# Latent attention in pairs of query blocks, with a split of the turned weights, in a two-block transformer kernel

## The reference, cut to what matters

```python
MLA_HEADS = 8; QK_NOPE = 64; QK_ROPE = 32; V_DIM = 64; Q_RANK = 256; KV_RANK = 128; Q_BLOCK = 128
def mla_attention(c_q, c_kv, k_rope, q_norm_g, w_uq, kv_norm_g, w_ukv, cos, sin):
    q = (rms_norm(c_q, q_norm_g) @ w_uq).reshape(b_, l_, MLA_HEADS, QK_NOPE + QK_ROPE)
    q_nope, q_rope = jnp.split(q, [QK_NOPE], axis=-1)
    q_rope = apply_rope(q_rope, cos[:, None, :], sin[:, None, :])
    kv = (rms_norm(c_kv, kv_norm_g) @ w_ukv).reshape(b_, l_, MLA_HEADS, QK_NOPE + V_DIM)
    k_nope, v = jnp.split(kv, [QK_NOPE], axis=-1)
    k_rope = apply_rope(k_rope, cos, sin)
    # k = [k_nope, k_rope shared by all heads]; q scaled by 96 ** -0.5
    # per query block: causal scores over all keys (the meta tokens too), softmax, times v
y_b = (mla_attention(cq, ckv, kr, ...) * jax.nn.silu(mg)) @ w_out_mla
```

## Time and profile before

| | before |
|---|---|
| median of 3 runs | 2844.04 us (2843.68 to 2848.91) |
| the profiled execution | 2843.15 us |
| its span, first to last instruction | 2841.3 us |
| busy: PE, weight loads (PEld) | 2760.0 us (97%), 2267.9 us (80%) |
| busy: DVE, ACT, POOL | 1026.0, 924.8, 578.6 us |
| mean granted TensorE clock | 0.991 |

### The profile page before, as it was taken

One profiled execution on the slowest core, in us unless ns is written; L12 is line 12 of the kernel. 1 busy time (PEld: TensorE's weight loads), 2 busy tenths in 40 slices (PEclk: granted clock), 3 DMA queues, 4 the chain that ended last, 5 costly groups with the idle time before them and its releaser, 6 DMA issues.

```text
span 2841.3 us, 34234 instructions
## 1 busy us (share of the span) xinstructions
PE 2760.0 (97%) x13644; PEld 2267.9 (80%) x13644; DVE 1026.0 (36%) x1293; ACT 924.8 (33%) x1477; POOL 578.6 (20%) x245
## 2 busy tenths in 40 slices
PE   7999999999999999999999999989999999999999
PEld 6677788898888888777778888867688888888887
DVE  3544423552323222734533665321333212121223
ACT  4455532112212114533434555332432112021122
POOL 1000012222222223221111224231121222222221
PEclk9999999999999999999999999999999999999999
DMA  3000001111111114131112123220021111111112
GB/s 125 14 13 13 15 22 45 51 46 39 43 52 48 46 48 148 38 106 38 38 37 87 46 86 131 100 67 30 23 66 38 45 52 45 52 44 52 45 52 89
DMA packets 42774, 154.50 MB, mean 54 GB/s; under 512 B 4884, under 2 KB 5204, under 8 KB 41896
## 3 DMA queue, kind: packets, MB, share of 16 engines
q1 hardware_dynamic: 37712, 128.11, 14.3%
q10 hardware_dynamic: 4952, 24.82, 2.3%
HBM read 138.04 MB, written 10.67 MB: 52 GB/s over the span
## 4 chain that ended last, share of the span: by engine, by line
PE 87%; DVE 5%; issue 4%; ACT 2%; POOL 1%; DMA 0%; ACTq 0%; DVEq 0%; POOLq 0%
PE ps L594 46%; PE ps L675 18%; PE ps L696 5%; PE ps L799 3%; PE ps L770 2%; PE ps L1108 2%; PE ps L1066 1%; PE ps L788 1%; PE ps L1269 1%; PE ps L1060 1%; DVE fx_tl L2531 1%; PE ps L653 1%; PE ps L1145 1%; PE ps L617 1%; PE ps L1175 1%
## 5 line engine op out<-in xcount | busy, mean ns | idle before, releaser
L506 POOL TENSOR_TENSOR w_lo<-w_raw,w_hi 128x1024 fp32r<-128x1024 f32 x205 | 500.7, 2443 | 2128.2 <-ACT w_hi L1369 2128.1
L594 PE MATMUL ps<-A_hi,w_hi 128*128 128x512 f32 (+1 forms) x1920 | 549.2, 372 | 9.0 <-POOL w_lo L506 3.1
L594 PE MATMUL ps<-A_lo,w_hi 128*128 128x512 f32 (+1 forms) x1920 | 544.7, 370 | 0.0
L594 PE MATMUL ps<-A_hi,w_lo 128*128 128x512 f32 (+1 forms) x1920 | 544.5, 370 | 0.0
L594 PEld LDWEIGHTS ps<-A_hi,w_hi 128*128 128x128 f32 x1920 | 342.1, 189 | 73.2 <-issue 6.2
L594 PEld LDWEIGHTS ps<-A_lo,w_hi 128*128 128x128 f32 x1920 | 343.3, 188 | 61.6
L594 PEld LDWEIGHTS ps<-A_hi,w_lo 128*128 128x128 f32 x1920 | 343.0, 188 | 61.6
L1369 ACT ACTIVATE w_hi<-w_raw 128x1024 fp32r<-128x1024 f32 x205 | 216.2, 1055 | 497.3 <-PE ps L675 342.7
L2599 DVE TENSOR_TENSOR X<-ps,X 128x512 f32<-128x512 f32 x96 | 66.4, 692 | 383.8 <-PE ps L675 305.9
L675 PE MATMUL ps<-w_hi,U_hi 128*128 128x512 f32 x448 | 174.3, 389 | 0.0
L675 PE MATMUL ps<-w_lo,U_hi 128*128 128x512 f32 x448 | 174.3, 389 | 0.0
...
## 6 DMA issues: line engine op xcount, KB each, us to landing
...
```

The lines of the kernel that those rows point to most:

```text
L506: nc.gpsimd.tensor_tensor(w_lo[:, slot, :], w_raw[:, slot, :], w_hi[:, slot, :].bitcast(F32), ALU.subtract).then_inc(w_lo_ready, 1)
L594: last = nc.tensor.matmul(out, w[:, slot, o:o + m], v[:, k, cols] if k is not None else v[:, cols], start=(first and j == 0 and q == 0), s ...
```

## The change

The loop over pairs of heads is written out as 8 heads of 4 steps (`MX_J`), each step a pair of query blocks (2j, 2j+1), j in the order 3, 0, 2, 1.

- Scores stay F32, over 128 rows instead of 96. The query projection, both halves of the rotary part and the scale are taken in one DVE instruction (rows 64 to 127 times cos and ±sin, rows 0 to 63 times 1); the keys hold their rotary part twice, in rows 64 to 95 and 96 to 127, so that the product itself adds the two halves. The mask is a product of an identity with a mask tile on PE. The meta keys stand behind the block's own keys for the first block of a pair, which makes products of 16 columns.
- The turned weights (10 chunks of 512 columns a head) are split into `mx_th` (ACT) and `mx_tl` (DVE), and are the moving operand of the value products, 256 columns for two query blocks; `mx_vs` = [V high|V low] is the stationary one, in fp32r. DVE adds the two halves (`mx_take`). The output comes out turned, so `turn_output` goes.
- The reciprocal of the sums goes through a row, two DMAs (SP) and a product on POOL with the Silu of the gate.
- The projections of the next head, the next pair's values and the gate stand as filler in the steps (`mx_fill`), in one PSUM bank (7) and one free corner (bank 1). The gate comes in two halves of 512 columns, so its Silu is taken in two places a pair.
- A new unit `mla_meta` holds the weights for all meta keys and meta values, which are multiplied once. The keys of a head are one accumulated product over two shifted slices of the weights.
- Elsewhere semaphores are merged; no instruction is changed there but for the slots' parity.

```diff
-    ("mla_heads", 4, (768, 1024)),
+    ("mla_meta", 1, (1024,)),
+    ("mla_heads", 1, (1024,) * 8),
...
+MX_J = (3, 0, 2, 1)
+MX_FIRST = (0, 4, 5, 8)
+MX_CHUNKS = 11
+MX_P_AT = {3: 0, 0: 1968, 2: 0, 1: 1968}
+MX_T_AT = {3: 0, 0: 4, 2: 0, 1: 3}
...
+    for _key in ([("key", 2 * _i + 1), ("query", 2 * _i + 1, 0), ("gate", _i)]
+                 + ([("key", 2 * _i + 2), ("query", 2 * _i + 2, 0), ("query", 2 * _i + 2, 1), ("value", _i + 1, 0), ("value", _i + 1, 1)]
+                    if _i < 3 else [])):
...
+        mx_k = ar("mx_k", 61696, [P, 2, S + 64])[:, :, 64 - META:S + 64]
+        mx_p = ar("mx_p", 70400, [P, 2912])
+        mx_vs = ar("mx_vs", 82176, [P, 2, 10, P], F32R)
+        mx_o = ar("mx_o", 92416, [P, S])
+        mx_th, mx_tl = xr("mx_th", 0, [P, 5, HB], F32R), xr("mx_tl", 10240, [P, 5, HB], F32R)
+        mx_q = xr("mx_q", 20480, [P, 2, S])
+        mx_sil = xr("mx_sil", 28672, [P, S])
...
+                def inverse(h):
+                    rows = slice(64 * (h % 2), 64 * (h % 2) + 64)
+                    sp.wait_ge(mx["row"], h + 1)
+                    sp.dma_start(inv_d[h % 2], mx_row[0:ST, h % 2, :]).then_inc(mx["inv_out"], 16)
+                    sp.wait_ge(mx["inv_out"], 16 * (h + 1))
+                    if h >= 2:
+                        sp.wait_ge(mx["si"], h // 2)
+                    sp.dma_start(mx_inv[rows, :], inv_d[h % 2].rearrange("q p -> (q p)").rearrange("(a c) -> a c", a=1)
+                                 .to_broadcast([64, S])).then_inc(mx["inv_in"], 16)
...
+            lows(0, n0 + 2)
+            for i in range(4):
+                mx_value_low(2 * i)
+                if i:
+                    silu_scaled(i - 1)
+                mx_value_low(2 * i + 1)
+                low(n0 + 2 * i + 2, (n0 + 2 * i + 2) % 2)
+                low(n0 + 2 * i + 3, (n0 + 2 * i + 3) % 2)
+            silu_scaled(3)
...
+            def mx_key(h, bank):
+
+
+                n, e = n0 + 2 * (h // 2), h % 2
+                pe.wait_ge(w_lo_ready, n + 1)
+                for hb in (1, 0):
+                    o, cols = 512 + 128 * e + 64 * (1 - hb), slice(META + hb * HB, META + hb * HB + HB)
+                    for x, (w, v) in enumerate(((w_hi, ckv_hi), (w_hi, ckv_lo), (w_lo, ckv_hi))):
+                        last = nc.tensor.matmul(ps[:, bank, :], w[:, n % 2, o:o + P], v[:, cols], start=(hb == 1 and x == 0),
+                                                stop=(hb == 0 and x == 2))
+                last.then_inc(mx["fd"], 1)
...
+                if h % 2 == 0:
+                    table = ((key, query(0, 7, (mx["v"], 2 * i + 2))), (none, gate(0, 0)), (query(1, 1), gate(0, 1)), (none, gate(1, 0)))
+                    if i == 3:
+                        table = (table[0], (none, none), (query(1, 1), none), (none, gate(0, 0)))
+                elif i < 3:
+                    table = ((key, gate(1, 1)), (none, query(0, 7, (mx["sil"], 2 * i + 2))), (query(1, 1), value(0)), (none, value(1)))
+                else:
+                    table = ((none, gate(0, 1)), (none, gate(1, 0)), (none, gate(1, 1)), (none, none))
+                return table[s]
...
+                for ab in range(2):
+                    qb = 2 * j + ab
+                    qs = slice(qb * P, (qb + 1) * P)
+                    n, flat = (qb + 1) * P, ps[:, 2 * ab:2 * ab + 2, :].rearrange("p a b -> p (a b)")
+                    if ab == 0:
+                        parts = [(c, META + c, min(HB, n - c)) for c in range(0, n, HB)] + [(n, 0, META)]
+                        d = qb * P
+                    elif j < 3:
+                        parts = [(c, c, min(HB, n + META - c)) for c in range(0, n + META, HB)]
+                        d = META + qb * P
+                    else:
+                        parts = [(c, META + c, HB) for c in range(0, n, HB)]
+                        d = qb * P
+                    for at_, c, w in parts:
+                        x, y = max(at_, d), min(at_ + w, d + P)
+                        last = nc.tensor.matmul(flat[:, at_:at_ + w], mx_q[:, e, qs], mx_k[:, e, c:c + w], start=True, stop=x >= y)
+                        if x < y:
+                            last = nc.tensor.matmul(flat[:, x:y], mx_ident[:, :], mx_future[:, x - d:y - d], start=False, stop=True)
...
+                whole = [(kb, t) for kb in range(2 * j + 1) for t in (mx_th, mx_tl)]
+                for x, (kb, t) in enumerate(whole[:1] + [(kb, t) for kb in ("own", "meta_a", "meta_b") for t in (mx_th, mx_tl)] + whole[1:]):
+                    end = MX_T_AT[j] + j
+                    if kb == "own":
+                        v, w, out = mx_vs[:, e, 2 * j + 1, :], t[:, end, 256:384], ps[:, 6, r0 + P:r0 + 256]
+                    elif kb == "meta_a":
+                        v, w, out = mx_vs[:, e, 8, :], t[:, end, 384:512], ps[:, 6, r0:r0 + P]
+                    elif kb == "meta_b":
+                        v, w, out = mx_vs[:, e, 9, :], t[:, end, 384:512], ps[:, 6, r0 + P:r0 + 256]
+                    else:
+                        cols = slice((kb % 2) * 256, (kb % 2) * 256 + 256)
+                        v, w, out = mx_vs[:, e, kb, :], t[:, MX_T_AT[j] + kb // 2, cols], ps[:, 6, r0:r0 + 256]
+                    last = nc.tensor.matmul(out, v, w, start=(x == 0), stop=(x == len(whole) + 5))
+                last.then_inc(mx["pv"], 1)
...
+            mx_scores(0, 0)
+            for h in range(HEADS):
+                for s in range(4):
+                    j = MX_J[s]
+                    behind_scores, at_end = mx_fill(h, s)
+                    mx_turn(h, s, range(0, min(2, j + 1)))
+                    if s < 3:
+                        mx_scores(h, s + 1)
+                    elif h + 1 < HEADS:
+                        mx_scores(h + 1, 0)
+                    if j >= 2:
+                        mx_turn(h, s, (2,))
+                    behind_scores()
+                    if s or h:
+                        mx_values(*((h, s - 1) if s else (h - 1, 3)))
+                    if j >= 3:
+                        mx_turn(h, s, (3,))
+                    if s == 3:
+                        mx_row_turn(h)
+                    at_end()
...
+            def mx_early(h, s):
+
+                i, odd = h // 2, h % 2
+                if s == 0 and not odd and i:
+                    mx_value_take(i, 1, 7)
+                    mx_value_high(h)
+                if s == 1 and not odd:
+                    mx_value_high(h + 1)
+                if s == 1 and odd:
+                    mx_silu(i, 0 if i == 3 else 1)
+                    if i < 3:
+                        after(n0, 0, 8, 2 * i + 1)
+                if s == 2 and not odd and i:
+                    mx_high(i - 1)
+                if s == 3 and not odd:
+                    if i < 3:
+                        mx_silu(i, 0)
+                    after(n0, 0, 8, 2 * i)
+                if s == 3 and odd:
+                    if i < 3:
+                        mx_value_take(i + 1, 0, 7)
+                    else:
+                        mx_silu(3, 1)
+                        after(n0, 0, 8, 7)
...
+                    mx_turned(h, s, range(0, min(2, j + 1)))
+                    mx_early(h, s)
+                    if following[0] < HEADS:
+                        mx_probs(*following, 0)
+                    if j >= 2:
+                        mx_turned(h, s, (2,))
+                    if following[0] < HEADS:
+                        mx_probs(*following, 1)
+                    if j >= 3:
+                        mx_turned(h, s, (3,))
+                    if s == 3:
+                        mx_row_copy(h)
+                    if s == 0 and h + 1 < HEADS:
+                        mx_key_take(h + 1, 1)
...
+                v.scalar_tensor_tensor(mx_q[:, e, cols], ps[:, bank, :], 96 ** -0.5, rope[:, META + cols.start:META + cols.stop],
+                                       ALU.mult, ALU.mult).then_inc(mx["q"], 1)
...
+                chain(v.tensor_copy(mx_low[own, k % 2, :], ps[other, 6, r0:r0 + 256]))
+                v.tensor_tensor(mx_o[own, j * 256:j * 256 + 256], ps[own, 6, r0:r0 + 256], mx_low[own, k % 2, :], ALU.add)\
+                    .then_inc(mx["o"], 1)
```

668 lines of the change are left out of this document (391 added, 277 removed).

## The result

| | before | after |
|---|---|---|
| median of 4 runs beside each other | 2843.86 us (2840.54 to 2848.91) | 2805.76 us (2803.48 to 2805.91) |
| ratio, 95% interval | | 0.9863 (0.9846 to 0.9880) |
| span of the profiled execution | 2841.3 us | 2804.0 us |
| busy: PE, PEld | 2760.0, 2267.9 us | 2724.0, 2251.2 us |
| busy: DVE, ACT, POOL | 1026.0, 924.8, 578.6 us | 1060.8, 926.4, 600.5 us |

A forecast was written before the change was run, and what follows sets the result against it. The prediction took PE (TensorE) to bound the kernel, with ACT and DVE beside it. Its terms summed to -19.4 us from the profiled 2843.15 us, 2823.8, given as a median of 2825 us; range 2810 to 2840 for 8 in 10.

The forecast's parts named there:

- Values: Latent attention's loop, value products on PE: shorter products at 0.12 and 0.13 us, -37.2 us, bounds -4 to +2.
- Rival 3: Value products gain nothing: short ones cost like 0.17 us each, masks 0.2; 2845 to 2849 us, chance 0.05.
- Transposes: Loop, transposes on PE including the output's: 48.1 us before, 38.9 after, -9.2 us, bounds ±4.
- Scores: Loop, scores on PE: F32 columns stay, added 16-column products at 0.22 us each cost +7.0 us.
- Masks: Loop, 72 mask products moved from DVE to PE at 0.15 us each: +10.8 us, bounds 0.06 and 0.20 each.
- Idle: PE's idle time in the loop: 14.4 us against 6.8, +7.6; 8 of it in the steps, bounds 0 and 18.
- Both ties: Odd head's second step, PE 7.6 us against ACT 7.4, and last step, 8.5 against 8.4; some tenths each.
- Projections, keys, meta unit: Loop, PE: queries, values' projection and gate nothing, keys -2 us, the new meta unit +2.6 us.
- Clock: Loop: one idle spell more lets the granted clock fall to its lower level, +1 us.
- Rival 1: ACT's table loads in Silu steps each cost one more of their own length: 14 us, 2839, chance 0.07.
- Rival 2: The chain of scores, maximum, exponential, transpose and split bounds the loop's steps: 48 us idle, 2865, chance 0.07.
- Rival 4: Loop cheaper all round: no idle in steps (-8), masks 0.08 (-5), short products 0.11 (-4): 2808 us, chance 0.15.

The follow-up runs named there:

- Run 8: Changed kernel with the turned weights left in F32, one value product in place of two of high and low weights; median 2829.1 us.
- run 1: Changed kernel with the 72 mask products left out of PE and nothing in their place; median 2803.2 us.
- run 11: Changed kernel with the 16-column product of each step's first scores issued four times (96 products more); median 2831.4 us.
- run 12: Changed kernel with the mask product in F32 instead of rounded F32; median 2815.1 us.
- run 10: Changed kernel with the queries' rotary product on DVE done three times, two more in each of 16 takes; median 2814.3 us.
- run 5: Changed kernel with a 16-column Silu and exponential ahead of each of the 8 Silus, two more table loads each; median 2829.8 us.

## Where the prediction was right and where it failed

**What bounds the kernel: right.** PE ended the loop before and after, and 36.9 of the 37.3 us of the span are the loop's; the parts ahead of it and behind it moved by +3.7 and -4.1 us.

**Values: right.** Predicted -37.2, measured -38.8; the products of 128 columns take 0.11 us, not the 0.13 taken, the lower of the bounds given. Run 8 shows that the gain has the two parts that its working implied. Rival 3 is out. How much is the values' and how much the masks' depends on the booking: without masks (run 1) the same value products take 57.0 us, not 53.1. Values, scores and masks together are firm: -26.1 measured, -19.4 in the sum.

**Transposes: -11.0 for -9.2**, within its bounds; they run at 0.11 us, not 0.12.

**Scores: the short products' price was right** (0.22 us each, run 11), the term was not. Without masks the scores take 71.2 us against 68.7 before, +2.5 for +7.0. By run 8's pace, 1.68 ns a column (45056 columns in 75.6 us), and 0.22 us a short product, the scores before should take 66.7 us (37632 columns and 16 short ones) and took 68.7, and after 72.9 (37120 and 48) and took 71.2. So 2 us are booked elsewhere on either side; that 64 pieces of scores became 32 is a candidate for the first, but none of this was tested, and these 4.5 us stay open.

**Masks: mis-sized, 0.15 taken, 0.09 measured** (runs 1 and 12), 4.5 us of the sum. I read the price from the starts around one record, and such a reading books on the mask part of the time of what stands behind it. The run without masks moved 3.9 us from masks to values in the same way.

**Idle: this is the step that failed.** "The forgetting attention, with the same structure and a filler in every step, has 8.4 us idle in 204 ... I take 8 us for the loop": marked in the steps are 0.57 us, in head 6. With the short waits, read from start to start, it is 2.4: 0.24 us ahead of the turn in three odd heads' second step, 0.23 for the copy of the keys four times, 0.8 in head 6. Start and end were right (3.6 and 1 predicted, 3.0 and 0.96 measured). Wrong was not the reading of the chain either. By the distances of the turns an odd head's second step has 7.01 us of work on PE and a chain of 7.25 (the sums had 7.6 and 7.4), its last step 8.04 and 7.94 (8.5 and 8.4), an even head's last 9.48 and 8.41 (10.0 and 8.6). Both ties are there, with an odd head's third step, which I had not called tight, as another (0.1 us, run 10); PE's sums were 0.5 us too high each. "A tie costs some tenths" held for the first tie, 0.24 us, and cost nothing in the second. Wrong was the step from there to 8 us: two ties in each of four odd heads at 0.3 us are 2.4, and the 8.4 us of the forgetting attention stand in another loop, with other work on the engines beside PE; no run shows that they bear on this one. What a tie costs here is the difference of its two sides and no average on top: the step of 7.25 us has that length to 0.01 us in each of heads 1, 3 and 5 of ten kernels, whether PE has 0.22 us less to do in it (run 1), 0.24 more (run 12), or the same.

**Projections, keys, meta unit:** within 1.3 us each. **Clock: right.** PE works 6.3 us of the loop at the lower clock (99.26 to 99.52 and 117.39 to 123.42), 3.9 us before, which is 1.2 us of time for the 1 in the sum; it is inside the rows of the table.

**Rival 1** (a drain on each table switch) is out. The rows of run 5 show four loads in one visit with ACT going on within 0.02 us of each one's end, and the 2.99 us that it adds are two loads and two short ACTIVATEs. The Trainium skill ("ScalarE: Activation LUTs", section "What ACT_TABLE_LOAD costs") has 2.66 us a switch; the measurement decides here. **Rival 2** (the chain becomes the bound) did not come as a whole, but in an odd head it is there in the second step and 0.1 us away in the next two: 3 us more on ACT in the second, or two more DVE products in the third, are paid in full or nearly so. **Rival 4** (2808) is where the result lies: little idle in the steps and masks at 0.09, two of its three reasons, and the third in part, as the values' 128-column products do run at 0.11.

**What would show it wrong:** L933 waited by far less than 1 us a step, masks took under 0.2 us, and outside the loop the sum changed by 0.4 us, so none of those signs came; the loop's 289 us was the number that failed, by 18.
